# Gate and up products of the last feed-forward stage: one PSUM bank for a chunk in place of two

## The reference

```
x = x + 0.5 * (silu(h @ w_gate) * (h @ w_up)) @ w_down      # h = rms_norm(x), F = 2816 hidden channels
...
return rms_norm(x, final_norm)
```

## Time and profile before

| what | us |
|---|---|
| median of 3 runs | 1125.18 (1125.0 to 1235.28) |
| profiled execution, its time | 1124.58 |
| its span | 1122.8 |
| TensorE busy | 1115.8 (99%), 8836 matmuls |
| weight loads of TensorE busy | 1074.9 (96%) |
| VectorE busy | 816.5 (73%) |
| ScalarE busy | 621.9 (55%) |
| mean DMA rate | 188 GB/s |
| granted TensorE clock | 0.999 of full speed |

### The profile page before, as it was taken

The page is one execution under the profiler, slowest core; times in us unless marked ns, Lnnn a source line. Parts: engine busy times, 40 slices in busy tenths (PEclk is TensorE's granted clock), DMA queues, the critical chain, the costliest instruction groups (busy, mean ns, idle before and its releaser), DMA issues.

```text
span 1122.8 us, 20773 instructions
## 1 busy us (share of the span) xinstructions
PE 1115.8 (99%) x8836; PEld 1074.9 (96%) x8836; DVE 816.5 (73%) x1144; ACT 621.9 (55%) x865; POOL 24.9 (2%) x50
## 2 busy tenths in 40 slices
PE   9999999999999999999999999999999999999998
PEld 8999999999899999999999999999999999888886
DVE  7766667899976775655686675579998768866764
ACT  6554555557765644544474554465667656644454
POOL 1000000100010000000000000010000100000000
PEclk9999999999999999999999999999999999999999
DMA  7965654554454366555547655545546444566551
GB/s 274 329 204 191 221 176 165 188 187 171 169 178 161 114 232 224 167 198 200 195 158 252 222 173 197 195 166 184 177 154 221 155 148 151 194 198 208 185 195 51
DMA packets 69932, 211.25 MB, mean 188 GB/s; under 512 B 5072, under 2 KB 28240, under 8 KB 65232
## 3 DMA queue, kind: packets, MB, share of 16 engines
q1 hardware_dynamic: 68864, 209.19, 54.6%
q10 hardware_dynamic: 976, 0.73, 0.2%
HBM read 208.85 MB, written 1.05 MB: 187 GB/s over the span
## 4 chain that ended last, share of the span: by engine, by line
PE 99%; DMA 0%; ACT 0%; DVE 0%; issue 0%; ACTq 0%; DVEq 0%
PE G L1903 10%; PE G L1902 10%; PE G L1904 10%; PE G L1928 8%; PE D L1724 8%; PE D L1731 8%; PE D L1723 8%; PE G L1936 4%; PE D L1844 2%; PE D L1845 2%; PE D L1846 2%; PE D L1770 2%; PE D L1768 2%; PE D L1769 2%; PE G L1844 2%; PE G L1846 2%
## 5 line engine op out<-in xcount | busy, mean ns | idle before, releaser
L1113 DVE TENSOR_TENSOR w_lo<-w_raw,w_hi 128x2048 fp32r<-128x2048 f32 (+3 forms) x260 | 452.3, 1746 | 108.8 <-ACT w_hi L683 108.0
L683 ACT ACTIVATE w_hi<-w_raw 128x2048 fp32r<-128x2048 f32 (+3 forms) x260 | 383.1, 1481 | 173.0 <-PE G L1904 112.8
L1902 PE MATMUL G<-a,w_hi 128*128 128x256 f32 x990 | 273.9, 277 | 0.3 <-DVE w_lo L1113 0.3
L1903 PE MATMUL G<-a,w_hi 128*128 128x256 f32 x990 | 273.5, 276 | 0.0
L1904 PE MATMUL G<-a,w_lo 128*128 128x256 f32 x990 | 273.5, 276 | 0.0
L1902 PEld LDWEIGHTS G<-a,w_hi 128*128 128x128 f32 x990 | 185.8, 188 | 0.8 <-DVE w_lo L1113 0.5
L1903 PEld LDWEIGHTS G<-a,w_hi 128*128 128x128 f32 x990 | 185.9, 188 | 0.0
L1904 PEld LDWEIGHTS G<-a,w_lo 128*128 128x128 f32 x990 | 185.9, 188 | 0.0
L1731 PE MATMUL D<-hT_hi,w_lo 128*128 128x256 f32 x528 | 145.7, 276 | 0.0
L1723 PE MATMUL D<-hT_hi,w_hi 128*128 128x256 f32 x528 | 145.7, 276 | 0.0
L1724 PE MATMUL D<-hT_lo,w_hi 128*128 128x256 f32 x528 | 145.7, 276 | 0.0
(11 more groups left out here) (303 smaller groups left out, 2073.2 us busy)
## 6 DMA issues: line engine op xcount, KB each, us to landing
w_raw<-w_dram SPq DMA_DIRECT2D x116, 1024.0 KB, 5.0
w_raw<-w_dram SPq DMA_DIRECT2D x151, 512.0 KB, 5.2
m_raw<-memT_dram SPq DMA_DIRECT2D x2, 1024.0 KB, 8.8
w_raw<-w_dram SPq DMA_DIRECT2D x6, 256.0 KB, 5.8
w_raw<-w_dram SPq DMA_DIRECT2D x8, 128.0 KB, 3.8
vx<-mem_dram SPq DMA_DIRECT2D x1, 1024.0 KB, 11.8
out_dram<-vx SPq DMA_DIRECT2D x3, 256.0 KB, 2.2
m_raw<-x_dram SPq DMA_DIRECT2D x2, 256.0 KB, 4.0
```

What stands on the lines that cost most here:

```text
L683: A(w_hi[:, part_hi(i)], w_raw[:, part(i)], ACT.Copy).then_inc(s_hi, 1)
L1113: V.tensor_tensor(w_lo[:, part_lo(i)], w_raw[:, part(i)], w_hi[:, part_hi(i)].bitcast(F32), ALU.subtract).then_inc(s_lo, 1)
L1902: M(out, whi[:, w], a_hi[:, k, :], start=(k, u) == (0, 0), stop=False, skip_group_check=True)
L1903: M(out, whi[:, w], a_lo[:, k, :], start=False, stop=False, skip_group_check=True)
```

## The change

In the last stage `by_twos` now holds for chunk 2 alone, so chunks 0, 1 and 3 to 21 take the one-bank function, with the bank rule and the shifted place of w_hi that the other stages have. The 21 copies (L775) and 21 sums (L1237) of these chunks go. `head_by_twos` and the form with the w_lo matmuls first are gone. The down products, the transposes and everything before the last stage are as they were.

```diff
 def by_twos(l, stage, c):
-    return last_stage(l, stage) or c == 2 or (l, stage, c) == (0, "ffn1", 5)
+    return c == 2 or (l, stage, c) == (0, "ffn1", 5)
 ...
     if stage in ("ffn1", "ffn2"):
-        return not (last_stage(l, stage) or (piece[0] == "gu" and by_twos(l, stage, piece[1])))
+        return not (by_twos(l, stage, piece[1]) if piece[0] == "gu" else last_stage(l, stage))
 ...
-        def two_banks(l, f, c):
-            return slice(0, 2) if last_stage(l, f"ffn{f + 1}") and c % 2 == 0 else slice(2, 4)
 ...
-                A(tail[:, :, :], GG[:, two_banks(l, f, c), T:], ACT.Copy).then_inc(s_tail, 1)
+                A(tail[:, :, :], GG[:, 2:4, T:], ACT.Copy).then_inc(s_tail, 1)
 ...
                     spread_inverse(l, f)
-                    if twos(l, f, 0):
-                        pair_sum(l, f, 0)
                     split(l, stage, ("gu", 3, 0, 8))
                     pair_scale(l, f, 0)
                     hidden(l, f, 0)
-                    if twos(l, f, 1):
-                        dve.drain()
-                        pair_sum(l, f, 1)
                     hidden_lo(l, f, 0)
 ...
-                elif last_stage(l, stage):
-                    for k in range(0, KD, 2):
-                        if k == 6:
-                            spread_mean_squares(q)
-                        head_by_twos(l, f, 0, range(k, k + 2), 8 * q, False)
-                        head_by_twos(l, f, 1, range(k, k + 2), None, True)
                 else:
                     for k in range(KD):
 ...
                 residual_by_token()
-                for c in range(2, STEPS):
-                    pe.wait_ge(s_sum, summed(l, f, c - 2))
-                    gate_up_by_twos(l, f, c, low_first=c % 2 == 1)
+                gate_up_by_twos(l, f, 2)
+                for c in range(3, STEPS):
+                    n = banks_freed_by(l, f, c)
+                    if twos(l, f, n):
+                        pe.wait_ge(s_sum, summed(l, f, n))
+                    else:
+                        pe.wait_ge(s_gu, chunk(l, f, n))
+                    gate_up(l, f, c, range(KD))
```

More of the change, by code:

```diff
@@ L818, in ffn @@
                     spread_root(l, f)
-                    if twos(l, f, 0):
-                        copy_tail(l, f, 0)
-                    if twos(l, f, 1):
-                        act.wait_ge(s_sum, summed(l, f, 0))
-                        copy_tail(l, f, 1)
                     silu(l, f, 0)
@@ L826, in ffn @@
                 for c in range(1, STEPS):
-                    if twos(l, f, c) and c > 1:
+                    if twos(l, f, c):
                         copy_tail(l, f, c)
@@ L1236, in pair_sum @@
                 dve.wait_ge(s_tail, summed(l, f, c))
-                V.tensor_tensor(gu[:, :, :], GG[:, two_banks(l, f, c), 0:T], tail[:, :, :], ALU.add
+                V.tensor_tensor(gu[:, :, :], GG[:, 2:4, 0:T], tail[:, :, :], ALU.add
                                 ).then_inc(s_sum, 1)
@@ L1906, in gate_up, with high_and_low @@
                     last.then_inc(s_blk, 1)
-            def high_and_low(l, f, c, ready=None, low_first=False):
-                banks = G[two_banks(l, f, c)]
+            def high_and_low(l, f, c):
+                banks = G[2:4]
                 whi, wlo = {}, {}
@@ L1923, in high_weights @@
                     for k in ks:
-                        if ready is not None:
-                            pe.wait_ge(s_alo, ready + k + 1)
                         both = a[:, k, :, :].rearrange("p a t -> p (a t)")
                         for b in range(2):
-                            last = M(banks[b], whi[k, b], both, start=k == 0 and not low_first, stop=k == KD - 1 and low_first,
-                                     skip_group_check=low_first)
+                            last = M(banks[b], whi[k, b], both, start=k == 0, stop=False)
                     return last
@@ L1935, in low_weights, with gate_up_by_twos @@
                         for b in range(2):
-                            last = M(banks[b][:, T:], wlo[k, b], a[:, k, 0, :], start=k == 0 and low_first,
-                                     stop=k == KD - 1 and not low_first, skip_group_check=low_first)
+                            last = M(banks[b][:, T:], wlo[k, b], a[:, k, 0, :], start=False, stop=k == KD - 1)
                     return last
                 return use, high_weights, low_weights
-            def gate_up_by_twos(l, f, c, low_first=False, middle=None):
-                use, high_weights, low_weights = high_and_low(l, f, c, low_first=low_first)
+            def gate_up_by_twos(l, f, c, middle=None):
+                use, high_weights, low_weights = high_and_low(l, f, c)
@@ L1945, in gate_up_by_twos @@
                 blocks = gate_up_blocks(l, f, c)
[L1946 to L1959, removed]
@@ L1960, in gate_up_by_twos @@
-                last.then_inc(s_blk, len(blocks))
[L1962 to L1973, removed]
+                for i, k0, k1 in blocks:
+                    use(i, k0, k1)
+                    for k in range(k0, min(k1, KD - 1)):
+                        if k == 2 and middle is not None:
+                            middle()
+                        high_weights(range(k, k + 1))
@@ L1975, in first_gate_up @@
+                low_weights(range(1))
+                high_weights(range(KD - 1, KD))
+                last = low_weights(range(1, KD))
+                last.then_inc(s_blk, len(blocks))
             def first_gate_up():
```

## The result

The changed kernel takes 1128.43 us (median of 7 runs, 1128.17 to 1130.37), the kernel before 1124.76 on the same occasions. The forecast was 1125.1 and its range ended at 1127.2, so it was wrong. The forecast also stood on a median of three runs of the kernel before, 1125.18; the median of seven is 0.4 us lower. The profiled execution took 1129.32 us, its span is 1127.6.

A forecast was written before the change was run, and what follows sets the result against it. TensorE's own stream alone was taken to bound the last stage. Head +0.17 and chunks 4 to 21 -0.24 sum to -0.07 us, giving 1125.1 us from a median of 1125.18; the range was 1123.9 to 1127.2.

The forecast's parts named there:

- What bounds: Last stage: only TensorE's own stream sets the time; the 21 copies and 21 sums are off the path, costed at nothing.
- Head: Chunks 0 and 1 and the mean square: 11.55 us like `ffn2` of layer 0, against 11.38, so 0.17 us more.
- Transposes, chunks 2 and 3: Last stage: transposes and chunk 2 unchanged, chunk 3 narrow with four width changes before and after; 0.
- Chunks 4 to 21: Nine pairs in the last stage, each with two width changes instead of four at 0.0135 us: 0.24 us less.
- two rows cited against rival 1: 30 narrow matmuls of a last-stage pair, behind 24 wide down products, hold 113.3 ns; 46 in the mixer, 113.5.
- rival 1: Chunks 3 to 21 keep the head's slow pitch, 117.9 against 113.3 ns: 4.2 us more, 1129.3; chance 9%.
- Down products: Last stage, the down products of two chunks: forecast 5.44 us, as before, so 0.
- Rival 2: Each matmul has a hidden fixed cost, at most 6.5 ns for 336 more: 2.2 us, 1127.3; chance 4%.

The follow-up runs named there:

- split kernel: Changed kernel with one wide token down matmul near the end of each group of down products split into two narrow ones: 1124.96 us, ratio 1.0001.
- test list: Unread test streams behind the last matmul, on the kernel before (w_hi unshifted), then the changed kernel (shifted); N48 behind R took 5.65, then 5.44 us.
- three splits: Changed kernel with one wide down matmul split near the group's end, 1124.96 us; at the group's start, 1129.01; the group's last matmul, 1128.57.

## Why the prediction was wrong

- **What bounds.** Right: TensorE alone, no wait before or after. Copies and sums were off the path, as priced.
- **Head**, +0.17: right, +0.16. It took the slow pitch of the other `ffn2` head. One reading was off: 64 of the 98 units of the old head are wide, not 48. Its narrow matmuls are at 118 ns (8 from 935.89 to 936.84), so the conclusion stood.
- **Transposes, chunks 2 and 3**, 0: right, -0.03.
- **Chunks 4 to 21**, -0.24, bounds -0.45 and 0: **this step failed.** It measured +3.4 us. The step priced the width changes and took the pitch of the runs between them from stages where each narrow run follows narrow down products. Here it follows 24 wide ones. In the kernel before, those were followed by 14 wide, 2 narrow, 2 wide and only then a long narrow run, which is the very order that leaves the fast pitch; one-bank chunks took it away. The two rows cited against rival 1 did not hold the case. The 30 narrow matmuls of the earlier trace rows do not stand directly behind the 24 down products but behind that order. And ahead of the 46 of the mixer stand 2 narrow and 2 wide ones as well, from 300.99 us. The gain of 0.24 itself would not have come at the fast pitch either: with shifted down products the pair took the forecast 10.91, but its group 5.49, 0.03 more for both together than before.
- **Down products**, 0: +0.2 us, each group 0.02 more. The first group, behind the fast chunk 3, has it too, so the slow pitch is not its reason; that it is the change of width now ahead of the group is not shown.
- **Rival 1** had the right pitch and nearly the right size (4.2 us, 1129.3), and 9%. Its mechanism was not what ran: it had the head's pitch kept from chunk 3 on, but chunk 3 was fast, and the slow pitch came in again behind the first down products. That its price is close is in part luck, 19 chunks in place of 18.
- **Rival 2**, a fixed cost per matmul, falls: chunk 3 went from 16 wide and 16 narrow to 48 narrow at 113.3 each, and the split kernel has 336 + 10 matmuls more at no cost. By the page "TensorE: Matmul & The Clock Gate" of the Trainium skill, section "Wait — 56ns, not 53.3ns?", matmuls start N / 2.4 GHz and about 2.5 ns apart, an estimated 109.2 ns for 256 columns. No row here shows that; the shortest steady pitch is 113.3 ns.
- The range should have reached rival 1, and it stopped short of rival 2's own price, 1127.3. Two pitches had been seen, and what chooses between them was not known.

What stays open is the mechanism in the engine. Shown is that the pitch follows from the order of widths, from the place of the weights in SBUF, and from the state ahead; that it is the same in every pair of a kernel, or in one case in every second pair; and that no work of the other engines is needed for it. A law that gives the pitch of any stream was not found: in the test list one wide matmul mends what two do not, and at another place the other way round.

## What to carry to other kernels

Where TensorE is the bound and waits for nothing, divide each stretch of the timeline by its matmuls before and after a change: a pitch 4% off is invisible in busy shares, waits and chain, and was 3.7 us here. A form taken over from another stage need not bring its pitch if what stands ahead of it, or where that work's weights lie, is different. If the pitch is off, split or insert one matmul near the entry and read the trace again. The place has to be tried: of three splits one helped, and a fix in one layer can cost time in the next. It can be worth it: 20 us hung on the order of four matmuls in each of the five two-bank chunks.

## What the runs showed of the hardware

- Back-to-back fp32r matmuls of 256 columns have two steady pitches in these kernels at the full granted clock, 113.3 and 117.8 ns. Either is kept for hundreds of matmuls and across down products: 1528 narrow matmuls at 117.8 with the two-bank chunks in plain order (589.07 to 769.03 us), 1526 at 113.3 in the kernel before (577.38 to 750.33).
- Where the weights lie changes the pitch of the narrow runs that read them. With w_hi not moved by its 16 elements (64 bytes) the pairs are at 117.8 ns and not 113.4. In the test list w_hi moved 48 elements further gave 117.7, and both parts moved so 120.0.
- In runs of 512 columns the place shows too, by up to 3%. The 24 down products take 5.44 us before (226.7 ns each) and 5.46 in the change with their weights unshifted, 5.49 with both parts shifted, 5.57 with w_lo alone and 5.59 with w_hi alone.
- fp32 matmuls and transposes can switch the pitch in either direction. Behind four of one column in the mixer it goes from 113.4 to 117.8 ns; behind two transposes of 128 in the mixer of layer 1 it goes back to 113.3.
